# Expert blocks of 128 rows become units of up to 288 rows, and the final norm moves into them

## The chip, the cores and the metric

The kernel runs on one core of a Trainium2 chip. The metric is the device time of one execution in microseconds (us); less is better. All arrays are float32 in DRAM. The core has TensorE (PE, with its weight loads listed apart as PEld), VectorE (DVE), ScalarE (ACT), GpSimd (POOL) and SyncE (SP), which only issues DMAs here. The engines run their own instruction lists in order and meet at semaphores.

## The reference, cut to what matters

One layer over 2048 prompt rows and 32 sample rows of 1024 numbers. A mixer part gives `h`; then each row goes to one of four groups and to two of the four experts in it:

```python
    hn = rmsnorm(h, g_ffn).reshape(B * L, D)
    y = h + hier_moe(hn, ...)            # per row: two experts of sixteen
    # an expert: silu(x @ w_gate[e]) * (x @ w_up[e]) @ w_down[e]; 1024 -> 512 -> 1024
    ...
    y_prompt = rmsnorm(hp, g_final)      # after the layer, over prompt and sample rows
    y_sample = rmsnorm(hs, g_final)
```

With the inputs of this case, the reference's routing sends these numbers of rows to the sixteen experts: 286, 252, 266, 258, 234, 249, 233, 272, 237, 251, 285, 249, 287, 254, 288, 259, together 4160.

## The kernel before, in words

`phase_one` is the mixer, the routing logits and the routing itself, in five passes over groups of 512 rows (the last one is the 32 sample rows). It leaves `h` and the normed rows `hn` in DRAM (`h_dram`, `hn_dram`), counts the rows of each expert in `running`, and writes each assignment's row number and weight into a table in DRAM (`slot_dram`) with indirect DMAs (L526).

`phase_three` is the experts. A float32 product is made of three products of float32r parts: each operand is split into a high half (ACT copies it, rounding) and a low half (DVE subtracts the high from the whole), and hi*hi, hi*lo and lo*hi are summed in PSUM. It loops over the experts and, inside, over an expert's blocks of 128 rows; the first block of an expert is written out apart (`peel`), because the weights are split while it runs. Per block:

- POOL copies the row numbers of the next block through small tiles (`idx`, L1403 to L1416), gathers its 128 rows of `hn` into `x` with an indirect DMA (L1411), and adds the weighted result of an earlier block to `h_dram` with an accumulating indirect DMA (L1419).
- PE transposes the rows (L1589), and multiplies with the rows as the stationary operand and the weights as the moving one (`accumulate`, L1597 to L1599): the gate, 8 x 3 matmuls of 512 columns; up, 2 x 8 x 3 of 256 columns; then the hidden rows are transposed (L1603) and multiplied with the down weights, 4 x 2 x 3 of 512 columns.
- ACT makes the sigmoid (L1483), the high halves (L1447, L1486, L1493) and the weighted result (`weigh`, L1457); DVE the products (L1562, L1565, L1570) and the low halves (L1507).
- SP loads the next expert's 6 MB of weights in three DMAs of 2 MB as soon as the raw tiles are free (L1367, L1370, L1373).

An expert has at least two blocks (`MINBLK`). `phase_four` then reads all rows of `h_dram` again, and per tile of 128 rows ACT sums the squares (L1703), DVE makes the mean (L1721), POOL the power of -1/2 (L1688), DVE the scaled row (L1716), and ACT issues the store (L1695).

`wait_apart` is a wait followed by an increment of a semaphore that nobody waits for, which keeps the wait an instruction of its own.

## Time and profile before

| | |
|---|---|
| time, median of 3 runs | 2057.92 us (2057.64 to 2058.57) |
| profiled execution, first to last instruction | 2054.1 us |
| busy PE, DVE, ACT, POOL | 1895.9, 1034.9, 832.3, 283.8 us |
| phase one, up to the first expert matmul | 1264.8 us |
| experts, first to last matmul | 732.6 us |
| last matmul to the end (last result added, final norm, stores) | 56.7 us |
| DMA: moved in all, mean rate | 316.24 MB, 154 GB/s |

The span is read from one profiled execution; the median of the timed runs is 3.8 us above it. Durations below are of single instructions in nanoseconds or microseconds as the profile gives them. A matmul's duration contains its pipeline, so the distance between two starts, not the duration, is what one costs on a busy PE.

### The profile page before, as it was taken

To read this page: it belongs to the slowest core of one execution; us is meant where nothing else is said; L and a number is where in the kernel's file an instruction comes from. 1 tells how busy PE (TensorE), PEld (TensorE's weight loads), DVE (VectorE), ACT (ScalarE), POOL (GpSimd) and SP (SyncE) were. 2 spreads that over 40 slices of the span, in tenths; PEclk is the share of its full clock that TensorE was granted. 3 is DMA by queue.
4 is the path that set the end of the run, shared out by engine and by line. 5 is a ranking of instruction groups with operands and counts; after the bars stand their busy time and mean duration, and the time that the engine had idled before them with its cause. 6 is when DMAs were issued, how large, how long until landed. Compare 5 with 4: busy or idle time off the path is not lost. (4 is left out here: it accounts for less than half of the span.)

```text
span 2054.1 us, 28746 instructions
## 1 busy us (share of the span) xinstructions
PE 1895.9 (92%) x9892; PEld 1600.8 (78%) x9893; DVE 1034.9 (50%) x2051; ACT 832.3 (41%) x1564; POOL 283.8 (14%) x388
## 2 busy tenths in 40 slices
PE   6999999999999999999997764999999999999980
PEld 5788888888878888888885543888888888888870
DVE  4644455544454544555444654454456454546434
ACT  4333333333343333333323553444446454446423
POOL 2000000010000010000100202222222222222223
PEclk9999999999999999999997886999999999999995
DMA  6332333323342223522334575585566576656428
GB/s 213 123 100 85 139 140 132 103 92 135 123 145 96 90 83 131 173 77 95 103 123 166 169 250 168 149 268 162 155 224 218 169 264 191 184 174 215 142 53 340
DMA packets 173306, 316.24 MB, mean 154 GB/s; under 512 B 9757, under 2 KB 92701, under 8 KB 173226
## 3 DMA queue, kind: packets, MB, share of 16 engines
q1 hardware_dynamic: 155754, 255.07, 36.0%
q0 software_dynamic: 15120, 51.59, 10.1%
q10 hardware_dynamic: 2352, 8.52, 1.0%
q8 instruction: 49, 0.80, 0.2%
q14 instruction: 31, 0.25, 0.0%
HBM read 266.09 MB, written 49.07 MB: 153 GB/s over the span
## 5 line engine op out<-in xcount | busy, mean ns | idle before, releaser
L751 DVE TENSOR_TENSOR wl<-raw,wh 128x512 fp32r<-128x512 f32 x440 | 274.3, 685 | 207.2 <-ACT wh L573 205.3
L1597 PE MATMUL bank<-gu_hi,ex_hi 128*128 128x256 f32 (+1 forms) x960 | 310.5, 323 | 4.5 <-DVE gu_lo L1507 4.5
L60 PE MATMUL bank<-xT_hi,wh 128*128 128x512 f32 x768 | 301.0, 392 | 10.6 <-ACT ext L711 7.0
L1599 PE MATMUL bank<-gu_hi,ex_lo 128*128 128x256 f32 (+1 forms) x960 | 307.1, 320 | 0.0
L1598 PE MATMUL bank<-gu_lo,ex_hi 128*128 128x256 f32 (+1 forms) x960 | 306.9, 320 | 0.0
L62 PE MATMUL bank<-xT_hi,wl 128*128 128x512 f32 x768 | 299.4, 390 | 0.0
L61 PE MATMUL bank<-xT_lo,wh 128*128 128x512 f32 x768 | 299.3, 390 | 0.0
L573 ACT ACTIVATE wh<-raw 128x512 fp32r<-128x512 f32 x440 | 240.2, 619 | 99.5 <-PE bank L1140 49.9
L1597 PEld LDWEIGHTS bank<-gu_hi,ex_hi 128*128 128x128 f32 x960 | 183.2, 191 | 23.9 <-DVE gu_lo L1507 6.5
L1599 PEld LDWEIGHTS bank<-gu_hi,ex_lo 128*128 128x128 f32 x960 | 183.2, 191 | 13.3
L1598 PEld LDWEIGHTS bank<-gu_lo,ex_hi 128*128 128x128 f32 x960 | 183.5, 191 | 12.5
L60 PEld LDWEIGHTS bank<-xT_hi,wh 128*128 128x128 f32 x768 | 144.6, 188 | 43.1 <-issue 8.2
L62 PEld LDWEIGHTS bank<-xT_hi,wl 128*128 128x128 f32 x768 | 144.5, 188 | 30.1
L61 PEld LDWEIGHTS bank<-xT_lo,wh 128*128 128x128 f32 x768 | 144.6, 188 | 29.8
L1507 DVE TENSOR_TENSOR gu_lo<-raw_gate_up,gu_hi 128x512 fp32r<-128x512 f32 x256 | 158.2, 685 | 2.0
L517 POOL TENSOR_TENSOR rs<-ms,half_neg 128x1 f32<-128x1 f32 (+1 forms) x51 | 34.0, 666 | 892.7 <-DVE ms L783 892.7
L1597 PE MATMUL bank<-dn_hi,hT_hi 128*128 128x512 f32 x320 | 134.0, 419 | 0.0
L1469 ACT ACTIVATE gu_hi<-raw_gate_up 128x512 fp32r<-128x512 f32 x240 | 128.2, 617 | 0.0
L1599 PE MATMUL bank<-dn_hi,hT_lo 128*128 128x512 f32 x320 | 125.6, 393 | 0.0
L1598 PE MATMUL bank<-dn_lo,hT_hi 128*128 128x512 f32 x320 | 125.6, 393 | 0.0
L636 ACT ACTIVATE S<-bank 128x512 f32<-128x512 f32 (+1 forms) x80 | 40.6, 517 | 200.3 <-PE bank L62 198.0
L1562 DVE TENSOR_TENSOR sg<-bank,sg 128x512 f32<-128x512 f32 x40 | 27.5, 689 | 181.4 <-ACT sg L1483 181.3
(239 smaller groups left out, 3258.0 us busy)
## 6 DMA issues: line engine op xcount, KB each, us to landing
raw<-in_w_in SPq DMA_DIRECT2D x70, 1024.0 KB
raw_gate_up<-in_w_gate SPq DMA_DIRECT2D x16, 2048.0 KB, 8.4
raw_gate_up<-in_w_up SPq DMA_DIRECT2D x16, 2048.0 KB, 13.4
raw_d<-in_w_down SPq DMA_DIRECT2D x16, 2048.0 KB, 13.0
raw<-in_w_out SPq DMA_DIRECT2D x20, 1024.0 KB
raw<-in_w_up_pool SPq DMA_DIRECT2D x20, 512.0 KB
raw<-in_w_up_gmlp SPq DMA_DIRECT2D x20, 512.0 KB
h<-in_x_prompt SPq DMA_DIRECT2D x16, 512.0 KB, 5.2
```

The costliest lines, as they stand in the source:

```text
L60: nc.tensor.matmul(out, lh, rh, start=(i == 0), stop=False)
L61: nc.tensor.matmul(out, lh, rl, start=False, stop=False)
L62: last = nc.tensor.matmul(out, ll, rh, start=False, stop=(i == n - 1))
L517: nc.gpsimd.tensor_tensor(rs[0:rows, col:col + 1], ms[0:rows, col:col + 1], half_neg[0:rows, :], ALU.pow).then_inc(done, 1)
L573: nc.scalar.activation(part(wh[par], q), part(raw[par], q), ACT.Copy).then_inc(w_hi, 1)
L636: nc.scalar.activation(S[:, 2 * kind + c, 0:n], bankA[b][:, 0:n], ACT.Sigmoid)\
L751: lo = lambda out, x, hi: tt(out, x, hi.bitcast(F32), ALU.subtract)
L1469: nc.scalar.activation(gu[0][:, k, :], raw_gu[:, k, :], ACT.Copy).then_inc(e_hi, 1)
L1507: lo_half = lambda out, a, hi: tt(out, a, hi.bitcast(F32), ALU.subtract)
L1597: nc.tensor.matmul(out, a[0][:, ka, :], w[0][:, kw, cols], start=(n == 0), stop=False)
L1598: nc.tensor.matmul(out, a[0][:, ka, :], w[1][:, kw, cols], start=False, stop=False)
L1599: return nc.tensor.matmul(out, a[1][:, ka, :], w[0][:, kw, cols], start=False, stop=(n == total - 1))
```

## The change

Routing: the slot table no longer has 128-row columns interleaved by row; each expert has a run of `SLOTS_PER_EXPERT` = 2304 slots, and an entry has five fields: row number, weight, and three row numbers to store to (or `NOWHERE`). Of a row's two experts the one with the lower number writes the sum so far back to `h_dram` (field 2), and the other writes the final output (field 3 for prompt rows, 4 for sample rows).

Experts: the loop runs over units. A unit is up to 288 rows of one expert: two tiles of 128 and a tail of 32. With the row counts above each expert has one unit, sixteen in all, where before there were 40 blocks. In a unit the gate and up weights are the stationary operand, in eight slices of 128 columns of the hidden layer (gate and up alternate), and the 288 transposed rows are the moving one; so the hidden values come out transposed, and the transposes of the hidden rows fall away. The slices are split into a ring of four buffers. For the down product a tile's hidden rows are stationary again; of the tail, the 32 high and 32 low halves are loaded as one stationary operand of 64 columns. The unit gathers its rows of `h_dram` too, adds the weighted result to them on DVE, squares, norms and scales them, and stores each tile three times (`h_dram`, `y_prompt`, `y_sample`), each with rows out of bounds dropped. `phase_four` is gone. Of the diff, the new lists of the five engines in `phase_three` stand below; what they replace is the code of the kernel before, shown above.

```diff
-BPE = (SEQ + SAMPLE + P - 1) // P
-NSLOT = NE * BPE
-MINBLK = 2
-MAXBLK = (2 * (SEQ + SAMPLE)) // P + MINBLK * NE
+TAIL = 32
+CAP = 2 * P + TAIL
+UPE = -(-(SEQ + SAMPLE) // CAP)
+SLOTS_PER_EXPERT = UPE * CAP
+NSLOT = NE * SLOTS_PER_EXPERT
+UNITS = 32
...
-            for rows in (h_dram, hn_dram):
-                pool.dma_start(rows[SEQ + SAMPLE:SEQ + SAMPLE + P, :], zero_rows).then_inc(spare_out, 16)
...
-                nc.vector.tensor_copy(low7[0:r, :, 0:nt], dest_f[0:r, :, 0:nt])
+                for c in range(2):
+                    stt(dest_f[0:r, c, 0:nt], rec[0:r, 0:nt, c], float(SLOTS_PER_EXPERT), dest_f[0:r, c, 0:nt],
+                        ALU.mult, ALU.add)
+                tt(later[0:r, 0:nt], rec[0:r, 0:nt, 0], rec[0:r, 0:nt, 1], ALU.is_gt)
...
+    TILES = [(0, P), (P, P), (2 * P, TAIL)]
+    ORDER = (0, 2, 1)
+    Y_OF = ((0, 1), (0, 1), (2, 3))
+    X_PARTS = [(0, 0), (0, 1), (1, 0), (1, 1), (2, None)]
...
             def _(sp):
...
+                    for t in range(3):
+                        sp.wait_ge(x_in[t], 16 * u + 16)
+                    sp.wait_ge(cur_ok, 2 * u + 2)
+                    load_slots(base)
+                    sp.wait_ge(w_lo, SLICES * u + SLICES - 1)
                     sp.dma_start(raw_gu[:, 0:KD, :], view(v["w_gate"])).then_inc(gate_in, 16)
+                    sp.wait_ge(w_lo, SLICES * u + SLICES)
                     sp.dma_start(raw_gu[:, KD:2 * KD, :], view(v["w_up"])).then_inc(up_in, 16)
+                    sp.wait_ge(d_lo, KH * u + KH)
                     sp.dma_start(raw_d[:, :, :], view(v["w_down"])).then_inc(down_in, 16)
...
             def _(pool):
...
+                def scatter(rows, frm, t, field, last, landed):
+                    n = TILES[t][1]
+                    nc.gpsimd.indirect_dma_start(out=rows, in_=frm[0:n, t, :], in_offset=None,
+                                                 out_offset=bass.IndirectOffsetOnAxis(
+                                                     ap=cur[0:n, t, field:field + 1], axis=0),
+                                                 bounds_check=last, oob_is_err=False).then_inc(landed, 16)
...
+                with pool.Fori(0, total) as u:
+                    nc.gpsimd.tensor_copy(cur[:, 0:2, :], nxt[:, 0:2, :]).then_inc(cur_ok, 1)
+                    nc.gpsimd.tensor_copy(cur[0:TAIL, 2, :], nxt[0:TAIL, 2, :]).then_inc(cur_ok, 1)
+                    wait_apart(pool, cur_ok, 2 * u + 2, passed_pool)
+                    gather(hrow, h_dram, cur, h_in)
+                    wait_apart(pool, x_tr, NX * u + NX, passed_pool)
+                    wait_apart(pool, slots_in, 32 * u + 64, passed_pool)
+                    gather(x, hn_dram, nxt, x_in)
+                    for i, t in enumerate(ORDER):
+                        n = TILES[t][1]
+                        wait_apart(pool, ms_ok, 3 * u + i + 1, passed_pool)
+                        nc.gpsimd.tensor_tensor(rs[0:n, t:t + 1], ms[0:n, t:t + 1], half_neg[0:n, :], ALU.pow)\
+                            .then_inc(rs_ok, 1)
+                        scatter(h_dram, hrow, t, 2, SEQ + SAMPLE - 1, h_back)
+                        wait_apart(pool, out_ok, 3 * u + i + 1, passed_pool)
+                        scatter(v["y_prompt"][0], out, t, 3, SEQ - 1, y_out)
+                        scatter(v["y_sample"][0], out, t, 4, SAMPLE - 1, y_out)
+                    wait_apart(pool, h_back, 48 * u + 48, passed_pool)
+                    wait_apart(pool, y_out, 96 * u + 96, passed_pool)
...
             def _(act):
...
+                with act.Fori(0, total) as u:
+                    for m in range(KH):
+                        act.wait_ge(gu_done, SLICES * u + 2 * m + 1)
+                        nc.scalar.activation(sg[m % 2][:, :], bankB[2 * (m % 2)][:, 0:CAP], ACT.Sigmoid).then_inc(sg_ok, 1)
+                        if m < 2:
+                            split(u, RING + 2 * m)
+                        if m == 0:
+                            act.wait_ge(down_in, 16 * u + 16)
+                        nc.scalar.activation(dn[0][:, m, :], raw_d[:, m, :], ACT.Copy).then_inc(d_hi, 1)
+                        act.wait_ge(hid_ok, KH * u + m + 1)
+                        nc.scalar.activation(H[:, m, 0:CAP], hid[m % 2][:, :], ACT.Copy).then_inc(H_hi, 1)
+                        if m < 2:
+                            split(u, RING + 2 * m + 1)
+                    rows_high(u + 1, 0)
+                    rows_high(u + 1, 1)
+                    split(u + 1, 0)
+                    rows_high(u + 1, 2)
+                    rows_high(u + 1, 3)
+                    square(u, 0)
+                    split(u + 1, 1)
+                    act.wait_ge(y_done, 3 * u + 2)
+                    for c, b in enumerate(Y_OF[2]):
+                        nc.scalar.activation(low[:, c * HALF:(c + 1) * HALF], bankY[b][TAIL:2 * TAIL, :], ACT.Copy)\
+                            .then_inc(low_ok, 1)
+                    rows_high(u + 1, 4)
+                    split(u + 1, 2)
+                    square(u, 1)
+                    split(u + 1, 3)
+                    square(u, 2)
...
             def _(dve):
...
+                def weigh(u, i):
+                    t = ORDER[i]
+                    n = TILES[t][1]
+                    dve.wait_ge(h_in[t], 16 * u + 16)
+                    dve.wait_ge(cur_ok, 2 * u + 2)
+                    if t < 2:
+                        dve.wait_ge(y_done, 3 * u + i + 1)
+                    else:
+                        for c, b in enumerate(Y_OF[t]):
+                            dve.wait_ge(low_ok, 2 * u + c + 1)
+                            tt(low[:, c * HALF:(c + 1) * HALF], bankY[b][0:TAIL, :], low[:, c * HALF:(c + 1) * HALF],
+                               ALU.add)
+                        dve.drain()
+                    for c, b in enumerate(Y_OF[t]):
+                        cols = slice(c * HALF, (c + 1) * HALF)
+                        last = stt(hrow[0:n, t, cols], bankY[b][0:n, :] if t < 2 else low[:, cols],
+                                   cur[0:n, t, 1:2].bitcast(F32), hrow[0:n, t, cols], ALU.mult, ALU.add)
+                    last.then_inc(y_read, 1)
+                def mean(u, i):
+                    t = ORDER[i]
+                    n = TILES[t][1]
+                    dve.wait_ge(sq_ok, 3 * u + i + 1)
+                    ts(ms[0:n, t:t + 1], ss[0:n, t:t + 1], 1.0 / D, EPS, ALU.mult, ALU.add).then_inc(ms_ok, 1)
+                def final(u, i):
+                    t = ORDER[i]
+                    n = TILES[t][1]
+                    dve.wait_ge(rs_ok, 3 * u + i + 1)
+                    stt(out[0:n, t, :], hrow[0:n, t, :], rs[0:n, t:t + 1], gf[0:n, :], ALU.mult, ALU.mult)\
+                        .then_inc(out_ok, 1)
...
+                with dve.Fori(0, total) as u:
+                    for m in range(KH):
+                        pair = 2 * (m % 2)
+                        dve.wait_ge(sg_ok, KH * u + m + 1)
+                        tt(sg[m % 2][:, :], bankB[pair][:, 0:CAP], sg[m % 2][:, :], ALU.mult).then_inc(g_read, 1)
+                        if m < 2:
+                            split(u, RING + 2 * m)
+                        dve.wait_ge(d_hi, KH * u + m + 1)
+                        minus(dn[1][:, m, :], raw_d[:, m, :], dn[0][:, m, :]).then_inc(d_lo, 1)
+                        dve.drain()
+                        dve.wait_ge(gu_done, SLICES * u + 2 * m + 2)
+                        tt(hid[m % 2][:, :], bankB[pair + 1][:, 0:CAP], sg[m % 2][:, :], ALU.mult).then_inc(hid_ok, 1)
+                        dve.wait_ge(H_hi, KH * u + m + 1)
+                        minus(H[:, m, CAP + TAIL:], hid[m % 2][:, 0:2 * P], H[:, m, 0:2 * P])
+                        minus(H[:, m, CAP:CAP + TAIL], hid[m % 2][:, 2 * P:], H[:, m, 2 * P:CAP]).then_inc(H_lo, 1)
+                        if m < 2:
+                            split(u, RING + 2 * m + 1)
+                    rows_low(u + 1, 0)
+                    rows_low(u + 1, 1)
+                    weigh(u, 0)
+                    split(u + 1, 0)
+                    rows_low(u + 1, 2)
+                    rows_low(u + 1, 3)
+                    mean(u, 0)
+                    split(u + 1, 1)
+                    final(u, 0)
+                    weigh(u, 1)
+                    rows_low(u + 1, 4)
+                    split(u + 1, 2)
+                    mean(u, 1)
+                    split(u + 1, 3)
+                    final(u, 1)
+                    weigh(u, 2)
+                    mean(u, 2)
+                    final(u, 2)
...
             def _(pe):
...
+                def down(u, t, ks):
+                    hi, lo = t * P, CAP + TAIL + t * P
+                    for k in ks:
+                        pe.wait_ge(H_lo, KH * u + k + 1)
+                        pe.wait_ge(d_lo, KH * u + k + 1)
+                        for c, b in enumerate(Y_OF[t]):
+                            half = slice(c * HALF, (c + 1) * HALF)
+                            last = three(bankY[b][:, :], (H[:, k, hi:hi + P], H[:, k, lo:lo + P]),
+                                         (dn[0][:, k, half], dn[1][:, k, half]), k == 0, k == KH - 1)
+                    return last
+                def down_tail(u):
                     for k in range(KH):
+                        for c, b in enumerate(Y_OF[2]):
+                            half = slice(c * HALF, (c + 1) * HALF)
+                            both = H[:, k, 2 * P:CAP + TAIL]
+                            nc.tensor.matmul(bankY[b][0:2 * TAIL, :], both, dn[0][:, k, half], start=(k == 0), stop=False)
+                            last = nc.tensor.matmul(bankY[b][0:2 * TAIL, :], both, dn[1][:, k, half], start=False,
+                                                    stop=(k == KH - 1))
+                    return last
...
+                with pe.Fori(0, total) as u:
+                    pe.wait_ge(x_lo, NX * u + NX)
+                    for s in range(SLICES):
+                        pe.wait_ge(w_lo, SLICES * u + s + 1)
+                        if s >= RING:
+                            pe.wait_ge(hid_ok if s % 2 else g_read, KH * u + s // 2 - 1)
+                        for k in range(KD):
+                            last = three(bankB[s % RING][:, 0:CAP],
+                                         (gu[0][:, s % RING, k, :], gu[1][:, s % RING, k, :]),
+                                         (xT[0][:, k, :], xT[1][:, k, :]), k == 0, k == KD - 1)
+                        last.then_inc(gu_done, 1)
+                    pe.wait_ge(y_read, 3 * u + 1)
+                    down(u, 0, range(3))
+                    pe.wait_ge(g_read, KH * u + 3)
+                    rows_of_x(u + 1, 0)
+                    pe.wait_ge(hid_ok, KH * u + 3)
+                    rows_of_x(u + 1, 1)
+                    down(u, 0, range(3, KH)).then_inc(y_done, 1)
+                    pe.wait_ge(hid_ok, KH * u + 4)
+                    rows_of_x(u + 1, 2)
+                    rows_of_x(u + 1, 3)
+                    down_tail(u).then_inc(y_done, 1)
+                    wait_apart(pe, x_lo, NX * u + NX + 1, passed_pe)
+                    rows_of_x(u + 1, 4)
+                    pe.wait_ge(y_read, 3 * u + 2)
+                    down(u, 1, range(KH)).then_inc(y_done, 1)
```

`split` is the high or the low half of one slice (128 x 1024), `rows_high` and `rows_low` those of four transposed 128 x 128 pieces (of the tail: eight of 128 x 32), `weigh` two operations of 512 columns that read PSUM and add to the gathered row (for the tail two additions more), `square` the sum of squares of 1024 columns, `final` the scaled output row. `gather` and `scatter` are three and one indirect DMAs. The units' experts and starts are worked out by some 30 small operations on DVE at the start of the phase, from `running`.

## Rows read from the trace of the kernel before

**Rows 1.** The page's first part: busy us, share of the span, instructions.

```profile
PE 1895.9 (92%) x9892; PEld 1600.8 (78%) x9893; DVE 1034.9 (50%) x2051; ACT 832.3 (41%) x1564; POOL 283.8 (14%) x388
```

**Rows 2.** Windows by stage: length, each engine's busy us, granted clock, DMA share, GB/s.

```profile
core 0: us, PE busy (x) PEld busy (x) DVE busy (x) ACT busy (x) POOL busy (x), PEclk, DMA share, GB/s
...
1240.00:1264.80 24.80, 1.94 (x8) 1.57 (x8) 6.91 (x23) 3.81 (x7) 7.52 (x20) 0.50 0.45 118
1264.80:1997.40 732.60, 732.53 (x4320) 640.30 (x4320) 379.41 (x614) 353.04 (x636) 173.91 (x238) 1.00 0.60 188
1997.40:2054.10 56.70, 0.00 (x0) 0.00 (x0) 22.99 (x34) 20.25 (x36) 20.62 (x19) 0.53 0.82 310
```

**Rows 3.** Waits of PE from 1264.8 us on: total, times, longest.

```profile
PE bank L1597 <- DVE gu_lo L1507: 4.5, 1, 4.5
```

**Rows 4.** Timeline of PE, one block: start us, duration us, instruction.

```profile
1501.03 0.40 PE L1597 MATMUL bank<-dn_hi,hT_hi 128*128 128x512 f32 x1
...
1504.44 0.40 PE L1597 MATMUL bank<-gu_hi,ex_hi 128*128 128x512 f32 x1
...
1509.94 0.28 PE L1597 MATMUL bank<-gu_hi,ex_hi 128*128 128x256 f32 x1
...
1515.33 0.40 PE L1603 MATMUL bank<-ident,hid 128*128 128x128 f32 x2
...
1515.93 1.04 PE L1589 MATMUL bank<-ident,x_rows 128*128 128x128 f32 x8
1516.94 0.49 PE L1597 MATMUL bank<-dn_hi,hT_hi 128*128 128x512 f32 x1
...
1522.99 0.39 PE L1597 MATMUL bank<-gu_hi,ex_hi 128*128 128x512 f32 x1
```

**Rows 5.** Groups of DVE by shape, from 1110 us on: busy us, mean ns.

```profile
L1507 DVE TENSOR_TENSOR dn_lo<-raw_d,dn_hi 128x1024 fp32r<-128x1024 f32 x64 | 76.8, 1221 | 7.7 <-ACT dn_hi L1477 6.2
...
L1507 DVE TENSOR_TENSOR hT_lo<-bank,hT_hi 128x256 fp32r<-128x256 f32 x80 | 33.8, 422 | 51.0 <-ACT hT_hi L1486 48.2
L1562 DVE TENSOR_TENSOR sg<-bank,sg 128x512 f32<-128x512 f32 x40 | 27.5, 689 | 181.4 <-ACT sg L1483 181.3
```

**Rows 6.** The instructions that touch `rs`: duration ns minimum, median, maximum.

```profile
L828 DVE SCALAR_TENSOR_TENSOR vf<-bank,rs,gv x17: 737/751/753, 42.2 to 1097.6; 128x512 f32<-128x512 f32 x16, 32x512 f32<-32x512 f32 x1
...
L1688 POOL TENSOR_TENSOR rs<-ms,half_neg x17: 541/1517/1581, 2016.4 to 2046.4; 128x1 f32<-128x1 f32 x16, 32x1 f32<-32x1 f32 x1
L1716 DVE SCALAR_TENSOR_TENSOR out<-final,rs,gf x17: 1261/1276/1285, 2017.1 to 2048.0; 128x1024 f32<-128x1024 f32 x16, 32x1024 f32<-32x1024 f32 x1
```

**Rows 7.** Groups of ACT by shape, from 1110 us on.

```profile
L1477 ACT ACTIVATE dn_hi<-raw_d 128x1024 fp32r<-128x1024 f32 x64 | 65.7, 1052 | 0.0
...
L1442 ACT ACT_TABLE_LOAD x16 | 20.5, 1283 | 20.2 <-issue 20.2
```

**Rows 8.** The instructions that touch `idx`, during the experts: durations, and time to landing.

```profile
L1403 POOL COPY idx<-idx x40: 185/185/1268, 1280.2 to 1991.8; 128x2 int32<-128x2 int32 x40
...
DMA to landing us min/median/max: 4.1/4.4/8.8
```

**Rows 9.** DMA issues: times, KB each, median us from issue to landing.

```profile
raw_gate_up<-in_w_gate SPq DMA_DIRECT2D x16, 2048.0 KB, 8.4
raw_gate_up<-in_w_up SPq DMA_DIRECT2D x16, 2048.0 KB, 13.4
...
h_rows<-h SPq DMA_DIRECT2D x16, 512.0 KB, 3.1
...
h_rows<-y_rows,idx_out POOLq DMA_INDIRECT x42, 9.1
```

**Rows 10.** Timeline of POOL: the idle time before an indirect DMA stands in brackets.

```profile
449.16 0.96 POOL L526 DMA_INDIRECT slot_table<-pay,dest  x1 [0.30 <-issue]
...
1500.98 0.99 POOL L1411 DMA_INDIRECT x_rows<-hn_rows,idx  x1 [0.84 <-POOL idx L1408]
```

**Rows 11.** The chain that ended last, in order of time: its longest piece.

```profile
2014.35 27.66 DMA final<-h_rows
```

More of the change, by code:

```diff
@@ L1377, in _ @@
[L1377 to L1380 removed]
+                wait_apart(sp, down_in, 16 * total + 16, passed_sp)
             @block.gpsimd
             def _(pool):
[L1386 to L1387 removed]
@@ new lines, in three @@
+                def three(to, a, w, first, final):
+                    nc.tensor.matmul(to, a[0], w[0], start=first, stop=False)
+                    nc.tensor.matmul(to, a[0], w[1], start=False, stop=False)
+                    return nc.tensor.matmul(to, a[1], w[0], start=False, stop=final)
+                def down(u, t, ks):
[8 more added lines that the diff above has]
+                    return last
```

549 lines of the change are left out of this document (186 added, 363 removed).

## The prediction

> **What bounds the kernel now.** I read the busy shares first, then windows by stage, because an average over a mixer, an expert loop and a tail says little. PE is busy 92% of the span [rows 1]. The stage table splits the span of 2054.1 us in three: 1264.8 us up to the first expert matmul (the mixer, of whose matmuls the change touches none), 732.6 us of experts, and 56.7 us with no matmul at all [rows 2]. During the experts PE is busy 732.5 of 732.6 us at a granted clock of 1.00 (the 2.4 GHz level), DVE 379, ACT 353, and the list of PE's waits has one entry, 4.5 us before the first matmul [rows 2, 3]. So the experts cost what PE's instruction list costs, and only fewer or shorter matmuls shorten them. The last 56.7 us are a load-bound tail: DMA is busy 82% at 310 GB/s, and the longest piece of the closing chain is 27.7 us of waiting for the rows of `h` [rows 2, 11].
>
> The price of a matmul is the distance between starts [rows 4]. From 1501.03 to 1504.44 there are 15 of 512 columns: 0.2273 us each. From 1509.94 to 1515.33 there are 45 of 256 columns: 0.1198 each. The difference is 0.42 ns a column (2.4 GHz) on 12 ns fixed. Eight transposes of rows take 1.01. One block takes 18.55 (1504.44 to 1522.99); the mean over 40 is 732.5 / 40 = 18.31. Built from these prices: gate 24 x 0.2273 = 5.46, up 48 x 0.1198 = 5.75, down 5.46, rows 1.01, and the two pairs of hidden transposes 0.24 each, 18.16; the list is 0.8% dearer than its prices.
>
> **The change on PE.** Each of the 16 experts has at most 288 rows, so 16 units stand for 40 blocks. Per unit:
> - gate and up: 8 slices x 8 x 3 = 192 matmuls of 288 columns. Not in the trace; between 256 (0.1198) and 512 columns the line gives 0.1198 + 32 x 0.00042 = 0.1332. 25.6 us. Bounds: 0.1198 (23.0) and 0.2273 (43.6); 288 is next to 256 and the slope is the clock's, so I take the line.
> - down, tiles 0 and 1: 48 x 0.2273 = 10.9. Tail: 16 x 0.2273 = 3.6, since its columns are 512 however few rows are stationary.
> - row transposes: 16 at 1.01 for eight = 2.0, and eight of 32 columns between nothing and 1.0; I take 0.6. Each return from transposes to matmuls costs about 0.1 [rows 4]: 0.3.
>
> 43.0 us, with 0.8% on top 43.4; 16 x 43.4 = 695, 38 us less than now. Per expert that is 43.4 against 2.5 x 18.31 = 45.8. The gain is small because the 288 padded columns replace 2.5 x 128 = 320 padded rows, and the tail's down product pays full width.
>
> The Trainium skill (TensorE: Matmul & The Clock Gate, "Wait — 56ns, not 53.3ns?") states N / 2.4 GHz + about 2.5 ns between starts for bf16, thus 122.5 ns for 288 columns. The trace does not agree for float32r: by that rule 256 columns would take 109 ns, and they take 119.8. By the rule the 192 matmuls would take 23.5 us, the units 33 us less in all.
>
> **The change on the others.** DVE per unit, in order of size: 8 slices and 4 pieces of the down weights at 1.221 = 14.7 [rows 5]; 3 final rows at 1.28 = 3.8 [rows 6]; rows' low halves 4 x 0.689 + 0.42 = 3.2; `weigh`: 6 at 0.751 and 2 additions at 0.69 = 5.9; gate and hidden products 8 at about 0.456 (288 between 256 at 0.422 and 512 at 0.689) = 3.6; hidden low halves 4 x (0.42 + 0.19) = 2.4; means 0.5 [rows 5, 6]. 34.1 of 43.4 us, so DVE's share rises from 52% to 79%. ACT: 15 pieces of 1024 at 1.052 (8 slices, 4 down, 3 squares) = 15.8, half of that for each of 6 pieces of 512 = 3.2, eight of 288 near 0.4 = 3.3, a table load of 1.28, about 24.5 [rows 7]. Both lie under PE while the order of the lists fits. I walked the five lists of one steady unit, each wait met at the later of the two times, with t = 0 at the start of the unit's first slice:
> - Slice 4 needs DVE's low half. DVE is still with the previous unit: it scales the last tile's rows until 9.2, then multiplies the gate and makes the low half by 10.9; PE wants it at 12.8. Slack 1.9.
> - The tail's rows for the next unit: PE ends the tail's down product at 37.0, ACT copies its low part to 38.3, DVE adds and weighs to 41.8 and makes the rows' low half by 42.3; PE wants it at 43.1. Slack 0.8.
> - Weights: SP issues them only after the slots, behind POOL's copies (17.1). Gate lands 8.4 after its issue at about 18, up 13.4 after [rows 9], near 27 and 34; ACT asks at 33 and 36. Down is issued when its low halves are done, at about 27, and is asked for in the next unit. Hidden; if each 2 MB took 1 us more, up would cost PE 1 us a unit.
>
> **The long chain is the rows' transport, and it hangs on POOL.** At t = 0 PE ended the previous unit's last down matmul. DVE is behind with the tail (low halves of two slices, a final row): it weighs tile 1 from 3.7 to 5.1; ACT's squares 6.4; mean 6.6; POOL's power between 0.54 and 1.58 [rows 6], taken 1.2: 7.8; final rows 9.2; POOL issues the store of y (0.84 before it, 0.96 for it [rows 10]), and it lands. A plain scatter with bounds is not in the trace: below stands a plain store of the same 512 KB, 3.1, above the accumulating scatter, 9.1 [rows 9]. I take 5.5, nearer to the plain one and with half the rows dropped: 15.8 with the third store. Then POOL may go on: two copies of the indices (0.19 free, 1.27 when blocked [rows 8]; 0.6 each) 17.1; three gathers of `h` with their gaps 21.7; the first gather of x starts at 22.8 and lands in 4.4 to 4.8 [rows 8]: 27.6. PE asks for it after eight slices and three quarters of a tile, at 29.7. Slack 2.1. Behind that wait stand PE's remaining down products, so all lateness beyond 2.1 goes one to one into the unit.
>
> Rows 8 show the copies at either 0.185 or up to 1.268, the length of one DVE operation on two SBUF tiles. The Trainium skill (SBUF — State Buffer, "Who interferes with whom") says that a DVE instruction with two SBUF inputs locks out a GpSimd instruction that reads SBUF; by that rule the three POOL operations of this chain could each cost a whole DVE operation, together 1.4 us more than I took, still inside the slack, and the sum would not change.
>
> Three slacks of 0.8 to 2.1 us on estimates of this kind will not all hold: I put 0.5 us a unit for them, 8 us. Experts: 703 us, 29.5 less.
>
> **Start of the experts.** Routing has some six small DVE operations more at the end of the last pass, +1 us; the zero rows' DMAs at the kernel's start, and the larger table that replaces them, lie beside the first loads. Then, now, PE idles to 1264.8 for slots, one gather, transposes, splits in a row. After, the splits of four slices go ahead of the rows. DVE sets: unit table about 8 us, four slices 4.9, rows 3.2, from 1244.4: 1260.5, with PE's wait for the last of it and the +1, 1262: 3 us less (bounds 6 less, 4 more). The half clock after it (0.50 [rows 2]) stays.
>
> **The tail.** Now 56.7. After: DVE weighs at 3.7 to 5.1 behind PE's end, final rows 9.2, the stores are issued by 12.3 and landed by 15.8, and about 1 us for the end: 17. 40 us less (bounds 14 and 21, by the landings). The table's reads of `h` (8.5 MB) are replaced by gathers within the units: experts move about 163 MB (17 x 6.3 of weights, 17 x 1.2 of x, 16 x 1.2 of h, 17 of stores) in 703 us, 232 GB/s, against 188 now; the tail shows that 310 can be moved [rows 2].
>
> **Sum.** 2054.1 - 29.5 - 3 - 40 = 1981.6; the median of the runs stands 3.8 above its profile's span: 1985 us.
>
> **Rivals.**
> - *The transport chain is a few us longer than its slack.* For: the stores' landing is unknown, POOL issues 15 indirect DMAs a unit where it issued 5 an expert, and DVE's share is 79%. With landings of 9.1 alone the chain is 3.6 longer, 1.5 to 2 over the slack: unit 45.4, total 2014. I give this case units of 44.8 to 48: 2005 to 2050.
> - *The same chain decides the sign.* The gain to lose is 72.5 + 8 = 80 us, 5.0 a unit, so the chain must be 7.1 longer than I worked it out. With landings of 9.1 (+3.6), gaps of 0.84 before all of the six indirect DMAs after the first (+3), x landing at 6 (+1.3), scatters issued at 1.6 each (+0.7) it is 8.6 longer: unit 49.9, total 2090. Against: back to back the gap is 0.30, and the 9.1 belongs to a scatter that reads and adds.
> - *A matmul of 288 columns costs what the column clock gives.* 0.1225 in place of 0.1332: 33 us less, 1952, if nothing else then binds; DVE's share would be 83% and I expect half of it to be lost. The skill's rule above is its ground; two spacings in rows 4 speak against it.
> - *More units than 16.* Two experts have 287 and 288 rows; one assignment that falls otherwise by rounding makes a seventeenth unit, 43.4 us with its own padding: 2028.
>
> **How the numbers follow.** Forecast (units 43.1 to 44.8; own range 1966 to 2004) 0.60; chain somewhat longer 0.24; chain decides the sign 0.08; column clock 0.04; a seventeenth unit 0.02; gains and losses that cancel 0.02. The range takes the forecast's and most of the second rival: 1962 to 2035. What a measurement of this kernel can tell from no change is about 0.2%, 4 us. Faster: 0.60 + 0.24 + 0.04 + 0.02 = 0.90; same 0.02; slower 0.08.
>
> **What the profile after would show.** PE: 16 x 192 matmuls of 288 columns 133 ns apart, a unit every 43 to 44.5 us, first matmul near 1262, 17 us behind the last. If I am wrong on the chain, PE's waits name DMA x_rows before the transposes, once a unit, of several us, with a granted clock that may fall behind them. If DVE is the wrong step, PE waits for the slices' or the tail rows' low half. If the landings are the step, the list of DMAs shows the stores over 7 us.

## The result

The changed kernel takes 1998.23 us (median; 1995.47 to 1998.7), the kernel before 2058.24 beside it: ratio 0.9706, 95% interval 0.969 to 0.9722. The forecast was 1985 with a range of 1962 to 2035. The sign and the range held; the point lay 13 us low. There are 16 units.

The page's first part of the kernel after, then its windows by stage, which answer to [rows 1] and [rows 2]:

```profile
PE 1859.0 (93%) x10068; PEld 1587.1 (79%) x10068; DVE 1145.8 (57%) x2186; ACT 808.2 (40%) x1424; POOL 418.3 (21%) x434
```

```profile
core 0: us, PE busy (x) PEld busy (x) DVE busy (x) ACT busy (x) POOL busy (x), PEclk, DMA share, GB/s
1240.00:1271.50 31.50, 7.15 (x36) 5.32 (x36) 19.38 (x75) 8.25 (x12) 10.32 (x12) 0.53 0.42 146
1271.50:1978.60 707.10, 690.13 (x4480) 620.94 (x4480) 496.69 (x743) 340.74 (x523) 319.86 (x306) 1.00 0.61 218
1978.60:1996.80 18.20, 0.00 (x0) 0.00 (x0) 7.19 (x10) 3.25 (x5) 10.16 (x9) 0.62 0.16 58
```

The experts take 707.1 us (forecast 703), the end 18.2 (17), and the first expert matmul stands at 1271.5 (1262). PE is no longer busy throughout: 690 of 707 us. Its list of waits during the units, where [rows 3] had one entry in front of them:

```profile
PE bank L1649 <- DVE ex_lo L1513: 17.7, 15, 1.4
PE bank L1644 <- issue: 0.2, 1, 0.2
```

Fifteen waits of 1.2 us on average, all in front of a unit's first matmul (one of them in front of the very first unit, where no unit runs yet), all for the low half of the x rows; the tail's piece is the last of them. No wait for x rows from DMA, none for a weight slice. One unit begins at 1581.05, the next at 1625.49. The timeline between them, SyncE's issue of the up weights and then what ScalarE, VectorE and PE do last:

```profile
1601.98 0.37 SPq L1402 DMA_DIRECT2D raw_gate_up<-in_w_up  x1
...
1618.85 1.06 ACT L1457 ACTIVATE gu_hi<-raw_gate_up 128x1024 fp32r<-128x1024 f32 x1 [2.89 <-DMA raw_gate_up<-in_w_up]
1619.93 1.07 ACT L1500 ACTIVATE tail_low<-bank 32x512 f32<-32x512 f32 x2
...
1619.94 1.23 DVE L1513 TENSOR_TENSOR gu_lo<-raw_gate_up,gu_hi 128x1024 fp32r<-128x1024 f32 x1 [2.78 <-ACT gu_hi L1457]
1621.09 1.28 DVE L1589 SCALAR_TENSOR_TENSOR out<-h_sum,rs,gf 128x1024 f32<-128x1024 f32 x1
1622.28 1.27 DVE L1570 TENSOR_TENSOR tail_low<-bank,tail_low 32x512 f32<-32x512 f32 x2
1623.63 1.40 DVE L1575 SCALAR_TENSOR_TENSOR h_sum<-tail_low,slots_now,h_sum 32x512 f32<-32x512 f32 x2
1624.96 0.40 DVE L1513 TENSOR_TENSOR ex_lo<-bank,ex_hi 128x256 fp32r<-128x256 f32 x1
...
1625.49 0.39 PE L1649 MATMUL bank<-ex_hi,gu_hi 128*128 128x288 f32 x1 [1.30 <-DVE ex_lo L1513]
```

Read it upwards. PE waits 1.30 for the tail rows' low half, in front of which VectorE has worked without a gap since 1619.94; there it had been idle 2.78 us, behind a ScalarE that had been idle 2.89 us, until the up weights had landed: 16.9 us after their issue, where the forecast took 13.4 from [rows 9]. The tail needs nothing of the up weights. It only stands behind them in two lists. The page's chain, of which PE takes 34% where PE is the bound (the first experiment), begins here with the transfer:

```profile
DMA raw_gate_up<-in_w_up 13%; ACT gu_hi L1457 3%; DVE gu_lo L1513 3%; DVEq L1607 1%; DVEq L1572 1%; DVE out L1589 1%; DVE tail_low L1570 1%; DVE h_sum L1575 1%; DVE dn_lo L1513 1%; POOL out L1423 1%; DVE hid L1609 1%; PE bank L1649 1%; PE bank L1651 0%; PE bank L1650 0%; DMA x_rows<-hn_rows,slots_next 0%
```

Why the landing is late stands in the windows of the same unit:

```profile
core 0: us, PE busy (x) PEld busy (x) DVE busy (x) ACT busy (x) POOL busy (x), PEclk, DMA share, GB/s
1581.05:1592.05 11.00, 10.97 (x82) 10.98 (x83) 8.26 (x11) 5.04 (x8) 8.12 (x8) 1.00 0.06 16
...
1602.05:1613.05 11.00, 11.00 (x69) 9.87 (x67) 5.86 (x12) 3.65 (x7) 3.02 (x3) 1.00 1.04 354
1613.05:1620.05 7.00, 7.00 (x41) 4.87 (x40) 4.22 (x8) 3.85 (x7) 1.62 (x2) 1.00 1.04 384
```

The mean of 218 GB/s hides two parts: 16 GB/s for the first 11 us, and all 16 DMA engines busy at 354 to 384 GB/s for the 18 us in which the gate, the up and the down weights and the gathers are in flight together. The Trainium skill (DMA: Bandwidth & Descriptors, "Where 436 GB/s comes from") puts the HBM limit of a core near 358 GB/s; the first of the two windows (354) agrees, the second (384) lies above it, and the measured rates are the ones used here.

The gate's landing, over the eleven units between 1400 and 1900 us, where [rows 9] had 8.4:

```profile
raw_gate_up<-in_w_gate SPq DMA_DIRECT2D x11, 2048.0 KB, 14.3
```

### The profile page after: what moved, and what is told of

It reads as the page before. It is cut to its first block and busy times, and to the rows that moved or that the text cites. A ratio compares the mean times of both kernels' runs of the same rounds, so it can differ in the third digit from the quotient of the medians.

```text
span 1996.8 us, 28344 instructions
## 1 busy us (share of the span) xinstructions
PE 1859.0 (93%) x10068; PEld 1587.1 (79%) x10068; DVE 1145.8 (57%) x2186; ACT 808.2 (40%) x1424; POOL 418.3 (21%) x434
## 5 line engine op out<-in xcount | busy, mean ns | idle before, releaser
L1649 PE MATMUL bank<-ex_hi,gu_hi 128*128 128x288 f32 x1024 | 304.4, 297 | 17.7 <-DVE ex_lo L1513 17.7
L1650 PE MATMUL bank<-ex_lo,gu_hi 128*128 128x288 f32 x1024 | 302.1, 295 | 0.0
L1651 PE MATMUL bank<-ex_hi,gu_lo 128*128 128x288 f32 x1024 | 301.1, 294 | 0.0
L1649 PEld LDWEIGHTS bank<-ex_hi,gu_hi 128*128 128x128 f32 x1024 | 191.8, 187 | 23.7 <-issue 23.7
L1513 DVE TENSOR_TENSOR gu_lo<-raw_gate_up,gu_hi 128x1024 fp32r<-128x1024 f32 x132 | 160.7, 1219 | 65.0 <-ACT gu_hi L1457 65.0
L1651 PEld LDWEIGHTS bank<-ex_hi,gu_lo 128*128 128x128 f32 x1024 | 192.8, 188 | 0.0
L1650 PEld LDWEIGHTS bank<-ex_lo,gu_hi 128*128 128x128 f32 x1024 | 192.2, 188 | 0.0
L1457 ACT ACTIVATE gu_hi<-raw_gate_up 128x1024 fp32r<-128x1024 f32 x132 | 138.4, 1051 | 41.2 <-DMA raw_gate_up<-in_w_up 41.2
L1144 PE MATMUL bank<-wh,mg_hi 128*128 128x512 f32 (+1 forms) x272 | 107.1, 394 | 3.7 <-DVE h L811 2.2
L1146 PE MATMUL bank<-wh,mg_lo 128*128 128x512 f32 (+1 forms) x272 | 106.0, 390 | 0.0
## 6 DMA issues: line engine op xcount, KB each, us to landing
raw_gate_up<-in_w_gate SPq DMA_DIRECT2D x17, 2048.0 KB, 14.3
```

The costliest lines, as they stand in the source:

```text
L1144: nc.tensor.matmul(out, ah, wh4, start=(n_acc == 0 and k == 0), stop=False)
L1457: nc.scalar.activation(gu[0][:, s % RING, :, :], slice_of(s), ACT.Copy).then_inc(w_hi, 1)
L1513: minus = lambda to, a, hi: tt(to, a, hi.bitcast(F32), ALU.subtract)
L1649: nc.tensor.matmul(to, a[0], w[0], start=first, stop=False)
L1650: nc.tensor.matmul(to, a[0], w[1], start=False, stop=False)
L1651: return nc.tensor.matmul(to, a[1], w[0], start=False, stop=final)
```

## The experiments

Two theories for the wait. A: the up weights' landing, through the order of the two lists. B: the chains through VectorE or POOL are themselves too long.

**The up slice behind the tail.** In ScalarE's list the split moves behind the tail's copies and rows, in VectorE's behind the final row, the weighing and the tail rows:

```
 ACT:                                 DVE:
     square(u, 0)                         mean(u, 0)
-    split(u + 1, 1)                 -    split(u + 1, 1)
     <low copies of the tail>             final(u, 0); weigh(u, 1)
     rows_high(u + 1, 4)                  rows_low(u + 1, 4)
+    split(u + 1, 1)                 +    split(u + 1, 1)
     split(u + 1, 2)                      split(u + 1, 2)
```

> The split of the first up slice of the next unit stands behind the tail's rows, on ScalarE and VectorE, instead of ahead of them. Theory A (the up weights' landing holds ScalarE at that split, and the tail's path stands behind it; that is PE's 1.4 us wait a unit for the tail rows' low half): ScalarE's wait for the up weights no longer stands ahead of the tail; PE's wait at the unit's first matmul falls below 0.4 us, the unit from 44.35 to 43.2 or 43.4; 16 units give 15 to 19 us: about 1981 us. Rival B (the tail's path through VectorE is itself too long, whatever the weights do): the same wait remains, 1998 us within 3. Rival C (the wait moves: the up slice is then late for PE's second slice): PE waits for a slice's low half in place of the tail rows', the gain is under 6 us, 1993 to 1998.

1975.73 us (1971.25 to 1981.17), ratio 0.9597 (0.9581 to 0.9613). Windows, PE's waits and the page's chain:

```profile
1270.60:1957.50 686.90, 686.80 (x4480) 624.44 (x4480) 498.21 (x745) 340.96 (x526) 345.60 (x307) 1.00 0.64 225
1957.50:1974.10 16.60, 0.00 (x0) 0.00 (x0) 5.54 (x8) 1.15 (x2) 9.59 (x8) 0.57 0.09 32
```

```profile
PE bank L1649 <- DVE ex_lo L1513: 1.0, 1, 1.0
```

```profile
PE bank L1649 10%; PE bank L1651 10%; PE bank L1650 10%; PE bank L1644 2%; PE bank L1670 1%; PE bank L1669 1%; DMA x_rows<-hn_rows,slots_next 0%; DVE gu_lo L1513 0%; POOL out L1423 0%; POOL rs L1442 0%; POOL h_rows L1423 0%; DVE ex_lo L1513 0%; DMA slots_next<-slot_table 0%; ACT ex_hi L1462 0%; DVE h_sum L1575 0%
```

The only wait left is the one in front of the first unit. Unit starts stand 42.81 us apart in 13 of 15 cases. The units give 20.2 us, the time 22.5, a little more than the 15 to 19 expected. The up weights land as before (16.8 us after their issue in the median; here and below a landing is the time of a DMA's last signal in the trace, which the page's list tells only where no signal is missing). So theory A is shown; nothing was made faster, two lines moved.

**More bytes ahead of the up weights.**

```
    sp.dma_start(raw_gu[:, 0:KD, :], view(v["w_gate"]))
+   sp.wait_ge(more_in, ...)       # the one of the unit before, landed long ago
+   sp.dma_start(more, <256 KB of the gate weights once more>)
    sp.wait_ge(w_lo, SLICES * u + SLICES)
    sp.dma_start(raw_gu[:, KD:2 * KD, :], view(v["w_up"]))
```

> One more load of 256 KB a unit on SyncE's queue between the gate's and the up's (8 rows of each partition of the gate weights once more, into a tile that nothing reads). Theory A (up's landing sets the unit's length): at the 216 GB/s that the units move, 256 KB are 1.2 us; up lands 1 to 1.5 us later and the whole of it goes into the unit: 16 x 1.2 = 19 us more, 2012 to 2022. Rival B (the landing is hidden, the tail's path through VectorE sets the length): ScalarE's wait for up grows by the 1.2 us, PE's does not: 1998 within 4.

2007.85 us, 9.6 more. In the profile PE's wait for the tail rows' low half grows from 17.7 to 24.0 us and the units take 720.3 instead of 707.1: 0.8 us a unit more. By the starts of units 2 to 16 it is 0.7 a unit; the rest is half clock in the first and in the last unit, 1.5 to 1.8 us each, which this profile has and the one of the changed kernel has not. By the trace's landings the up weights land at 38.5 in the unit instead of 37.8. Direction and place are A's; the size is under the expected 12 to 22 us, for I had priced the bytes at the mean rate. At the 354 to 384 GB/s of the window in which they travel, 256 KB are 0.7 us.

**Fewer transports.** The three scatters to y_sample leave each unit, and y_sample is not written.

> The three scatters a unit to y_sample are left out, so that y_sample is not written; their queue's work on POOL is three DMAs of 12 a unit. Theory A (POOL's chain of transports has slack; the up weights' landing sets the unit): POOL's busy time falls by 3 to 4 us a unit, the indices are copied 1.3 us earlier, PE's waits stay as they are, 1998 to 1992 us. Rival B (the rows' transport chain through POOL sets the unit, as the prediction's first rival had it): each y_sample scatter is 1.3 us on the chain, once a unit behind the last final row: 1998 - 16 x 1.3 = 1977 us.

2003.75 us, 5.5 more, where A had expected none to 6 less. The units take 711.1 us, PE's waits are 20.2 us for the same low half. So POOL's queue held nothing up. With POOL sooner through, the first gather of h starts 14.1 to 14.5 us into the unit in five of units 4 to 14 and at 15.6 to 15.9 in the other six (16.0 in the kernel after). In the five the gate lands 16.1 to 16.8 us after its issue, in the six 13.9 to 14.9 (14.1 to 14.9 in the kernel after), and the five units are 45.0 us long on average, the six 44.2. Gathers that fly beside the gate hold it up; two runs below that start the x gathers later show the other direction.

**The gate ahead of the slots.** SyncE issues the gate weights before it waits for the x rows and loads the slots:

```
+   sp.wait_ge(w_lo, SLICES * u + SLICES - 1)
+   sp.dma_start(raw_gu[:, 0:KD, :], view(v["w_gate"]))
    for t in range(3): sp.wait_ge(x_in[t], 16 * u + 16)
    sp.wait_ge(cur_ok, 2 * u + 2)
    load_slots(base)
-   sp.wait_ge(w_lo, SLICES * u + SLICES - 1)
-   sp.dma_start(raw_gu[:, 0:KD, :], view(v["w_gate"]))
```

> SyncE issues the gate weights as soon as their place is read, ahead of the waits for x rows and for the copied indices and ahead of the slots' load. Theory A (the issue of the up weights is set by VectorE's low half of slice 7, and it is their landing that counts): up is issued where it is now, 20.9 us into the unit; the gate, in flight at most 1.5 us earlier, takes a little less from it: 1998 to 1994 us. Rival B (the slots' wait, behind POOL's copies, holds the weights): gate and up are issued 1 to 2 us earlier and land so, 1998 - 16 x 1.2 = 1979 us. Later slots would show as a wait of POOL for them before the gathers of x, and as a PE wait for x rows.

2112.45 us: 114 more, which neither theory had; only the expectation's last sentence names the route. PE's waits, POOL's waits, and the list of DMA issues with the landings of the gate and of the two loads of slots:

```profile
PE bank L1644 <- DMA x_rows<-hn_rows,slots_next: 104.3, 15, 7.3
```

```profile
POOL x_rows L1417 <- DMA slots_next<-slot_table: 178.8, 16, 24.8
```

```profile
raw_gate_up<-in_w_gate SPq DMA_DIRECT2D x9, 2048.0 KB, 12.4
...
slots_next<-slot_table SPq DMA_DIRECT2D x9, 5.0 KB, 10.9
slots_next<-slot_table SPq DMA_DIRECT2D x9, 0.6 KB, 11.4
```

The slots are 5.6 KB and are issued 0.8 us behind the gate, at +16.5 in the unit, scarcely later than before (+15.3). But they land 11 us after their issue, with the gate's 2 MB, since they are behind it on the same queue; by the trace's landings the second of them took 1.5 us in the kernel after. The gathers of x start at +29 instead of +20, and PE waits 7 us a unit. The wait also costs clock. In the fifth unit PE starts again at 1507.2:

```profile
1507.20:1513.10 5.90, 5.87 (x23) 5.21 (x23) 2.71 (x5) 2.62 (x4) 0.00 (x0) 0.50 0.62 225
```

The granted clock is 0.50 (the 1.2 GHz level) for the 5.9 us behind the wait, with 512-column matmuls 427 ns apart, and such a spell stands behind each of the fifteen waits. The units become 52.0 us. With the gathers of x out of its way the gate lands after 12.4 us, where it took 14.3. The Trainium skill (same page, "Queues, rings and completion order") says that a DMA engine alternates between queues and that each takes the descriptors of one ring in their order; the two landings agree.

**The slack of the rows' transport.** On the late up split, POOL does three or six memsets between the gathers of h and those of x:

```
    gather(hrow, h_dram, cur, h_in)
+   for i in range(3):          # 6 in the second kernel
+       nc.gpsimd.memset(idle, 0.0)   # each waited for
```

> The order of the late up split, and three memsets of 128 x 1024 on POOL between the gathers of h and those of x, about 0.95 each (4 KB of a partition took 0.945 before), so that the x rows come 2.8 to 3 us later. It measures the slack of the rows' transport. Theory A (slack of the second tile's rows is near 0.5 to 1 us: its gather starts at 21.5 in the unit, takes 10, and PE asks at 32.1): PE waits some 2 us a unit for DMA x_rows, 16 x 2.1 = 34 us on 1975.7: 2005 to 2020, more if the clock falls behind the wait. Rival B (the prediction's slack of 2.1 us holds or is more): under 1 us a unit, 1976 to 1992.

> The same with six memsets, 5.7 us and their waits. Past its slack the chain should go into the unit one to one: against the kernel with three memsets 2.8 to 3 us a unit more, 45 to 48 us, if the clock stays at 1.00; the half clock after each wait of over 2 us, as in the kernel that loads the gate before the slots, would add 1 to 2 us a unit. Rival (two tiles' waits overlap with other slack, half goes in): 20 to 30 us more.

2003.79 us with three and 2071.2 in the one execution with six. PE's waits:

```profile
PE bank L1648 <- DMA x_rows<-hn_rows,slots_next: 26.8, 15, 2.1
```

```profile
PE bank L1648 <- DMA x_rows<-hn_rows,slots_next: 62.5, 15, 5.1
```

Three first, then six. The first gather of x starts 4.0 us later with three (23.7 in the unit instead of 19.7), and PE waits 1.8 us a unit, so 2.2 us of the delay are swallowed, where the forecast had a slack of 2.1. But the slack that stands in the kernel is not 2.2. PE asks for the first x tile at 29.85 (1610.90 in the unit shown above). By the trace's landings (medians of units 3 to 15) the gather lands at 29.1 with the late up split, 9.5 us after its issue, and at 31.5 with three memsets, 7.8 after: 0.7 us are slack, and the rest is that the gather which starts later flies for a shorter time. In the changed kernel itself it lands at 29.3 to 29.9, and next to nothing is left. The gate gains too: it lands after 12.1 us instead of 14.4, with only the x gathers moved. So gathers and weights do hold each other up.

With six, the waits grow by 36 us but the experts by 61 (721.2 to 782.1): the rest is the half clock, found behind each of these waits of 3.7 to 5.1 us and behind two of the fifteen waits of 1.6 to 2.1 us with three. The wait of some 2 us a unit was expected of the run with three, with a smaller slack and a shorter delay; the expectation for six, 2.8 to 3 us a unit more and 1 to 2 for the clock, held: 61 us over fifteen waits are 4.1.

**The norm behind the units.** Units as they are, sums written back by both experts, the last stage of the kernel before put back.

> The units stay and the final norm goes back behind them: both experts' sums are written back to h_rows, the squares, means, powers, final rows and y scatters leave the units, and the last stage of the kernel before is back. Theory A: the last stage costs what it did, 56.7 us behind the last matmul in place of 18.2, 38 us more; in the units the final row that stood on VectorE between the up slice and the tail rows (1.28 us) is gone, and with it PE's 1.2 us wait, 16 to 19 us less: 1998 + 38 - 17 = 2019 us (2012 to 2026). The change then is worth 39 us by its units and 21 by its norm. Rival B (VectorE's load is not what lets PE wait): the waits stay, 2036 us. Rival C (transports on POOL's queue hold the units now): without six scatters a unit the units fall to 42.8 and the end still costs 38: 2012.

2008.72 us, ratio 0.9752 (0.973 to 0.9774).

```profile
1269.80:1955.00 685.20, 685.17 (x4480) 623.13 (x4480) 447.04 (x654) 294.80 (x432) 190.32 (x170) 1.00 0.64 225
1955.00:2007.40 52.40, 0.00 (x0) 0.00 (x0) 24.39 (x36) 18.98 (x34) 20.06 (x19) 0.52 0.84 335
```

Units of 42.81 us without a wait, and an end of 52.4. So the units alone are worth 50 us, and moving the norm into them 10 more: it takes 34 from the end and gives 22 back in the units, by PE's waits. With the two lines of the late up split moved as well, the norm's move is worth 33 (2008.72 to 1975.73), since the units without the norm have no wait to lose.

The time is under the expected 2012 to 2026; I had taken 56.7 for the end and 17 for the waits. The wait was gone as expected, but not for the reason expected, the final row that VectorE no longer makes in front of the tail's rows. The up weights, from 1400 to 1900 us:

```profile
raw_gate_up<-in_w_up SPq DMA_DIRECT2D x12, 2048.0 KB, 15.6
```

They are issued 16.9 us into the unit instead of 20.9, because without the squares and the final row at the unit's start ScalarE and VectorE come to the slices sooner (the eighth low half is done at 16.9 instead of 20.9), and land near 32.5 instead of 37.8; ScalarE, which asked for them at 34.9, has no wait for a DMA left. That is the same cause as in the first experiment. What the missing final row adds, this run can't tell.

**The two kernels again, for second profiles of the mixer.**

> The changed kernel once more, for a second profile. Theory A (the 10 us by which the mixer ended later than in the profile of before are mostly chance, half-clock spells of 2 to 3 us that begin behind short waits in some executions and not in others): the last slots' scatter is again somewhere in 1241 to 1248, not the same to 0.3 us, with another set of spells. Rival B (the edit costs it): the same 1247 within 0.5 us, with the same spells.

> The kernel before once more, for a second profile of its mixer. Nine profiles of the changed mixer have their last slots' scatter between 1241.0 and 1247.2 us. Theory A (the edit itself costs about 4 us in the mixer, through VectorE's routing operations and where they lie, and the rest is chance): the mark is again 1236 to 1240. Rival B (all chance): it may be anywhere in 1237 to 1247.

Single times 1995.33 and 2061.38. The last scatter of slots, in the first profile of before, in the second, in the first of after and in the second:

```profile
L526 POOL DMA_INDIRECT slot_table<-pay,dest x2: 870/891/912, 1237.2 to 1238.4; - x2
```

```profile
L526 POOL DMA_INDIRECT slot_table<-pay,dest x2: 871/892/913, 1243.9 to 1245.1; - x2
```

```profile
L526 POOL DMA_INDIRECT slot_table<-pay,dest x2: 869/894/920, 1247.2 to 1248.5; - x2
```

```profile
L526 POOL DMA_INDIRECT slot_table<-pay,dest x2: 865/892/919, 1242.7 to 1243.9; - x2
```

All twelve profiles with the changed mixer lie between 1241.0 and 1247.2 (mean 1244.2), the two of before at 1237.2 and 1243.9. Half-clock spells (mostly seven or eight matmuls of 512 columns at 427 ns, 0.2 us longer each) come and go between executions. One at 24 us and those near 620 and 1090 are in all four profiles; besides, there are spells at 68, 314, 571 and 843 us in the first profile of after, and at 1211 and 1221 in the second. So two executions of the same kernel can differ by 7 us at this mark, and the 10 us between the first profiles were mostly chance. Whether the edit costs some us of them can't be said with two profiles of before.

**Towards a better kernel.** On the late up split, first the last tile's weighing ahead of slice 3 and the tail's final row; on that, the start of the experts (down weights and gains loaded behind the first x rows, VectorE's rows behind one slice instead of four); last, that start without the early weighing.

```
 DVE, early weighing:                 start:
     mean(u, 1)                           load_slots(0)
+    weigh(u, 2)                     +    for t in range(3): sp.wait_ge(x_in[t], 16)
     split(u + 1, 3)                      sp.dma_start(raw_d, ...); sp.dma_start(gf, ...)
     final(u, 1)                          ...
-    weigh(u, 2)                     -    DVE: split 0..3, rows_low 0..4, wait for gf
     mean(u, 2); final(u, 2)         +    DVE: split 0, rows_low 0..4, split 1..3
```

> On top of the late up split, VectorE weighs the unit's last tile ahead of the low half of slice 3 and of the tail's final row, so that the square, the mean, the power, the final row and the stores of the last tile follow sooner behind PE's last matmul. Expected: VectorE's final row of the last tile ends 8.3 us behind the last matmul now and 6.4 then; the units stay at 42.81, since slice 3 is asked for 9.6 us into the unit: 1975.7 - 1.9 = 1973.8 us. Rival: the slices' order becomes too tight at the unit's start and PE waits for a slice's low half, some tenths of a us a unit, 1976 to 1982.

> On top of that, the start of the experts: SyncE loads the down weights and the final gains behind the landing of the first x rows, VectorE takes the rows' low halves behind the first slice instead of behind the fourth. Theory: the gathers took 8.3 and 9.2 us beside the down weights and 4.7 in the kernel before, so the rows come 3.5 us sooner; VectorE's three other slices (3.5 us) go behind the rows, where PE takes 3.2 us for each slice: the first expert matmul some 3.5 to 4 us sooner behind the slots' load, about 13.7 us instead of 17.5, 1970 us. Rival (the gather does not depend on the load beside it): the rows come as now, 0.7 us is gained.

> The late up split and the early rows, without the early weighing, which made units of 42.8 to 43.4 us where the late up split alone had 42.81 in 13 of 15. Expected against the kernel with all three: the units 0.15 to 0.2 us shorter each, 2 to 3 us, and the same end or 0.6 less: 1969 us; against the late up split alone 4.1 us less. Rival (the variations of the units come from the start's other order, not from the early weighing): 1972.

The early weighing gave 1975.89, no gain: its end is 17.2 us. VectorE's final row of the last tile still waits for POOL's power, and POOL waits in its own order for the tail's final row, which the edit had put later. The early rows gave 1971.77 (1970 expected), with the first expert matmul 13.4 us behind the slots' load instead of 17.6: the first gather lands 4.5 us after its issue, where it took 8.5 beside the 2 MB of down weights and the 0.5 MB of gains. The late up split with the early rows, without the early weighing, is 1971.12 us (1968.93 to 1972.58), ratio 0.9573 (0.956 to 0.9586), 1.4% under the changed kernel; the units are back at 42.81 in all cases but two, so it was the early weighing that had lengthened them. The times alone can't tell this from the rival: the median lies between the two forecasts (1969 and 1972) and within the spread of the one before. Windows of this last kernel:

```profile
1265.00:1952.30 687.30, 687.22 (x4480) 625.15 (x4480) 501.52 (x748) 340.92 (x526) 345.77 (x307) 1.00 0.65 228
1952.30:1968.90 16.60, 0.00 (x0) 0.00 (x0) 5.54 (x8) 1.15 (x2) 9.60 (x8) 0.60 0.09 33
```

## Why the prediction was right, and where it was off

- **The price of a 288-column matmul: right.** Two groups of the timeline of the kernel after:

```profile
1601.17 0.30 PE L1649 MATMUL bank<-ex_hi,gu_hi 128*128 128x288 f32 x1
...
1606.77 0.40 PE L1649 MATMUL bank<-dn_hi,hidden_hi_lo 128*128 128x512 f32 x1
```

  There are 42 matmuls between these starts, 0.1333 us each; 0.1332 was taken. The column clock's 0.1225 did not come: that rival is out for this type.
- **PE's list: 0.6 us a unit too dear.** 43.4 was forecast, 42.81 measured where nothing waits. The prices alone gave 43.0; the 0.8% on top, read from the blocks of before, did not carry over. The experts without waits are 686.9 us, not 695.
- **The allowance for stalls: too small, and this is the term that failed.** 0.5 us a unit was put down; it is 20.2 us over the experts, 1.3 a unit, as the late up split shows. The step is "gate lands 8.4 after its issue, up 13.4 after": 14.3 and 16.9 were measured. The walk had the issue of up right (34 less 13.4 is 20.6; measured 20.9) and even the sentence that a slower load would cost PE one to one; ScalarE asks at 34.9, where it had 36. It took the landing from a kernel that moved 188 GB/s and checked the new load against a mean of 232, where the unit moves two thirds of its bytes in 18 us.
- **The tail rows' slack of 0.8 us: about right.** With the weights out of its way the low half is done at 1613.10 and PE asks at 1614.86, 1.76 us later; in the forecast's order the up slice's 1.22 stand in front of it, which leaves 0.5.
- **The rows' transport: no wait, as forecast, but two errors and luck.** The first gather of x starts at 20.2 instead of 22.8: a store of y lands 1.9 to 3.5 us after its issue where the trace tells it (the run without y_sample), and 5.5 was taken. The gather then takes 9.1 to 9.7 us instead of 4.8, the same crowded stretch as for the weights. It lands at 29.3 to 29.9, not at 27.6, and PE asks at 29.85: the 2.1 us of slack were not there. The first two rivals, which hung on this chain, did not come, because the two errors nearly cancel and because a gather that starts later is shorter (4.0 us of delay cost 1.8). The run with six memsets shows what the rivals would have been, and that the price is more than one to one once the clock falls.
- **VectorE at 34.1 of 43.4 us (79%)**: 496.7 / 16 = 31.0, 70%. The single durations were right (1.23, 1.28, 1.27 and 1.40 above), but neighbours overlap at their ends by about 0.1 us (1619.94 + 1.23 against 1621.09), and a sum of durations counts that twice. Not the bound in either case. ScalarE's sum is written as about 24.5, but its terms add up to 23.5; measured are 340.7 / 16 = 21.3.
- **The start: right in sum.** From the slots' load to the first expert matmul 17.4 us, where the forecast comes to 17.6 (1262 less 1244.4). VectorE's table and four slices took 12.6 us of the 12.9 forecast; its rows then stood partly behind the x rows, whose gather of 8.5 us the sum does not have, and the run with the early rows shows that 4 us could be had there. What lay under the start moved: the mixer of the one profile of before had ended early, and the sum inherited that.
- **The end: 18.2 for 17.**
- **The totals beside two rivals: too high.** On the prediction's own sum, units of 45.4 us give 2009 and not 2014, and units of 49.9 give 2081 and not 2090. No chance hangs on it.

The errors together: list -8, stalls +12, end +1, first matmul +9.5, and -2 because an execution's time lies 1.6 us above its span, not 3.8 (1998.45 for 1996.8; the profile of before was of one of the shorter ones): 12.5 of the 13.2 us.

## What to carry to other kernels

When weights are streamed once per unit, a mean rate says little about a landing: look at the DMA share in windows of a few us, and price a load at the rate of the window in which it flies. In an engine's list, put work that waits for a late transfer behind work that does not need it; here two moved lines were worth 22 us, while moving the norm brought 10 without them and 33 with them. Two small loads behind a large one on the same queue arrive with the large one.

One profile of the kernel before is one execution: a stage that the change does not touch can differ by 7 us between two of them, and a sum made against a single span inherits it.

## What was not expected of the hardware

- Slots of 5.6 KB, 0.8 us behind a 2 MB load on the same queue, took 11 us to land; the kernel lost 114 us to it.
- A gather of 512 KB on POOL's queue, beside 2.5 MB of loads on SyncE's, took 8.5 us instead of 4.5. Beside the gate and the up weights it took 9.1 to 9.7 us, and 7.8 when it started 4 us later; the gate's 2 MB then landed after 12.1 us instead of 14.4.
- Half-clock spells of about 3 us stand behind short waits of PE in the mixer, in some executions and not in others: a wait of 2.0 us near 67 us is in all fourteen profiles, a spell 1.3 to 1.9 us behind it in six. Behind two of fifteen waits of 1.6 to 2.1 us once a unit there was one, behind waits of 3.7 to 7.3 us each time, and with waits of 3.7 to 5.1 us the spells added two thirds of the waits' own growth (36 us of waits, 61 of time).
